# mLSTM products on quarters of the TensorE array in a two-block transformer kernel

## Chip, cores and metric

One Trainium2 chip, one of its cores. The metric is the device time of one execution in microseconds (us), the median of three; the trace is one more execution taken by the hardware profiler. TensorE (PE) does the matrix products, VectorE (DVE) and ScalarE (ACT) the element-wise work, SyncE (SP) and GpSimd (POOL) start transfers.

## The reference, cut to what matters

The program runs a first block of two layers (HGRN2 mixer, dilated attention, SwiGLU) and a second block of two hybrid layers on 512 tokens of width 1024. The change touches only the mLSTM mixer of the two hybrid layers. It has 4 heads, keys of width 64, values of width 128, and chunks of 64 tokens, so 8 chunks:

```
M_HEADS = 4; M_QK_DIM = 64; M_V_DIM = 128; M_CHUNK = 64
q, k, v = chunks(q) * (dk ** -0.5), chunks(k), chunks(v)
dC = einsum('bnhlv,bnhlk->bnhvk', v * e[..., None], k)        # update of each chunk
dn = einsum('bnhl,bnhlk->bnhk', e, k)
C_new = a[..., None, None] * C + s[..., None, None] * dC_c    # scan over the chunks
w = exp(log_d - m_t[..., None]) * einsum('bnhlk,bnhsk->bnhls', q, k)
num = einsum('bnhls,bnhsv->bnhlv', w, v) + a_inter[..., None] * einsum('bnhvk,bnhlk->bnhlv', C_prev, q)
den = sum(w, axis=-1) + a_inter * einsum('bnhk,bnhlk->bnhl', n_prev, q)
h = num / maximum(abs(den), exp(-m_t))[..., None]
```

Within a chunk the scores and weights are causal. Across chunks only the state C, n is used, so scores between tokens of different chunks are never needed.

## The kernel before

All work is written by hand, engine by engine, in plain order; semaphores tie the engines. The big weight products (`plain`, L2073) split every float32 operand into two parts of type fp32r and make three passes (`PASSES`); one step ("tick") is one 128x512 tile of PSUM tensor G over 4 k-blocks, 12 matmuls on line L2113 or L2117. Other PE work is hung into these ticks: `z_steps(T)` runs ahead of tick T and calls `window` (sliding-window attention) and `mlstm` (L2637). These small products write PSUM tensor X (four banks of 512 float32 columns) and are plain float32.

Head h of the mLSTM starts at tick 62 + 4h (`head_start`), and has stages at fixed distances from that tick (`heads_at(T, after)`), on PE:

- after 0: mask through the identity (L2662, bf16) and row maxima (L2665, fp32r) into X bank 0, 512 columns each ("exponents"); then the **scores**, L2668: four matmuls 128x128x128, keys by queries of 128 tokens, into bank 1. Two heads share the 128 rows of the key tile `tmp[:, 4 or 6, :]`. `q_alone` (DVE, L1854) multiplies the pair's queries by a column `q8` that is 1/8 on the own head's 64 rows and 0 on the other head's.
- after 1: decay rows into bank 0 (L2672). DVE multiplies weights with scores (L1873) and queries with decays (L1877).
- after 2: the **updates**, L2682: seven matmuls, 64 tokens of the chunk as contraction (array rows 0-63 for even chunks, 64-127 for odd ones), both heads' 128 key columns, 129 value columns. Even chunks go to bank 0 or 1 and odd ones to bank 2 (`m_bank`).
- after 3: DVE runs the scan over the chunks into `m_state` (L1883, L1886).
- after 4: the **output** into banks 2 and 3 (`out_view`). First the weighted values, L2651: four matmuls 128x129 over 128 tokens. Then the states, L2654: seven matmuls with all 128 rows as contraction and 64 query columns, on array columns 0-63 and 64-127 in turn.
- after 5: ACT squares the output (L1098), DVE makes the norm (L1894 to L1901); after 6 PE transposes (L2344); after 7 DVE finishes the head (L1907, "done").

Since head h+1 starts four ticks after head h, stage 4 of h and stage 0 of h+1 fall on the same tick; before the change the code puts the output first. `n.take(s)` waits for the next signal of another engine, `n.own(s)` for one's own, `n.give(ins, s)` makes `ins` signal.

Of the kernel before, what the change touches and what calls it, by code (L numbers as in the profile page):

```python
# [18 lines left out]
ALU = mybir.AluOpType  # L19
AX = mybir.AxisListType.X  # L20

P = 128
# [3 lines left out]
TB = S // P  # L26
# [19 lines left out]
def constants():  # L46

    r = np.arange(P)
    f = {}
# [12 lines left out]
    q8 = np.zeros((P, 2))  # L62
    q8[:64, 0] = q8[64:, 1] = M_DK ** -0.5
    f["q8"] = q8
# [119 lines left out]
def build(nc, a, out, where1, where2, where3, stop=None):  # L184
# [12 lines left out]
    with ctx:  # L197
# [49 lines left out]
        with ExitStack() as room:  # L247
# [46 lines left out]
                                             "output", "squares", "variance", "std", "normed", "transposed", "done")}  # L294
# [8 lines left out]
        ident, ones, halves, freq, sign, q8 = (c1(k) for k in ("ident", "ones", "half", "freq", "sign", "q8"))  # L303
# [83 lines left out]
        def keys_of(i):  # L387

            return (i - 1, i) if i else (0,)

# [838 lines left out]
        def _(dve):  # L1229
# [622 lines left out]
            def q_alone(h):  # L1852

                n.give(ts(tmp[:, 1, :], z_qm[:, h // 2, :], q8[:, h % 2:h % 2 + 1], None, ALU.mult), ms["q_alone"])  # L1854

            def k_end(h):
                pr = h // 2
                for j in range(TB):
                    ins = ts(tmp[:, 3, blk(j)], z_km[:, j, pr * P:(pr + 1) * P], mcol[:, 16 + 4 * j + h:17 + 4 * j + h], None, ALU.mult)
                n.give(ins, ms["k_end"])  # L1860

            def mlstm(T, l):
# [6 lines left out]
                for h in heads_at(T, 1):  # L1869
                    W = tmp[:, (0, 5)[h % 2], :]  # L1870
                    n.take(ms["weights_exp"])
                    n.take(ms["scores"])
                    n.give(tt(W, W, X[:, 1, :], ALU.mult), ms["weights"])  # L1873
                    qs = tmp[:, (2, 7)[h % 2], :]
                    n.take(ms["decay"])
                    n.own(ms["q_alone"])
                    n.give(tt(qs, tmp[:, 1, :], X[:, 0, :], ALU.mult), ms["q_decayed"])  # L1877
                    if h + 1 < M_HEADS:
                        n.own(ms["q_decayed"])
                        q_alone(h + 1)  # L1880
                for h in heads_at(T, 3):
                    n.take(ms["updates"])
                    link(v.tensor_copy(m_state[:, 0, :], X[:, 0, 0:P + 1]))  # L1883
                    for c in range(1, 7):
                        bank, i = m_bank(c)
                        ins = stt(m_state[:, c, :], m_state[:, c - 1, :], mcol[:, 48 + 8 * h + c:49 + 8 * h + c],  # L1886
                                  X[:, bank, (P + 1) * i:(P + 1) * (i + 1)], ALU.mult, ALU.add)
# [157 lines left out]
        def _(pe):  # L2045
# [591 lines left out]
            def mlstm(T):  # L2637
# [8 lines left out]
                for h in heads_at(T, 4):  # L2646
                    n.take(ms["states"])
                    n.take(ms["done"] if h else ws["done"])
                    W, qs = tmp[:, (0, 5)[h % 2], :], tmp[:, (2, 7)[h % 2], :]
                    for j in range(TB):  # L2650
                        mm(out_view[:, j, 0:P + 1], W[:, blk(j)], z_vm[:, j, h, :], start=j % 2 == 0, stop=False, skip_group_check=True)  # L2651
                    for c in range(1, 8):
                        r = slice(64 * (c % 2), 64 * (c % 2) + 64)
                        ins = mm(out_view[r, c // 2, 0:P + 1], qs[:, 64 * c:64 * c + 64], m_state[:, c - 1, :],  # L2654
                                 start=False, stop=c == 7, skip_group_check=True)
                    n.give(ins, ms["output"])
                for h in heads_at(T, 0):
                    pr = h // 2
                    if h == 0:
                        n.take(ms["columns_copied"])  # L2660
                        n.take(ms["k_copied"])
                    mm(X[:, 0, :], identb, mk("ml", 0, 512), start=True, stop=False)  # L2662
                    if h == 0:
                        n.take(ms["rows_selected"])
                    n.give(mm(X[:, 0, :], sel_max[:, blk(h)], rows_r[:, :], start=False, stop=True), ms["exponents"])  # L2665
                    n.take(ms["q_alone"])
                    for j in range(TB):
                        ins = mm(X[:, 1, blk(j)], tmp[:, (4, 6)[pr], blk(j)], tmp[:, 1, blk(j)], start=True, stop=True, skip_group_check=True)  # L2668
                    n.give(ins, ms["scores"])
                for h in heads_at(T, 1):  # L2670
                    n.take(ms["weights_exp"])
                    n.give(mm(X[:, 0, :], sel_decay[:, blk(h)], rows_r[:, :], start=True, stop=True), ms["decay"])  # L2672
                for h in heads_at(T, 2):
# [5 lines left out]
                    for c in range(7):  # L2679
                        r = slice(64 * (c % 2), 64 * (c % 2) + 64)  # L2680
# [141 lines left out]
```

## Time and profile before

| | us |
|---|---|
| median of three | 3033.14 |
| lowest, highest | 3032.38, 3034.7 |
| the profiled execution | 3033.12 |
| its span, first to last instruction | 3031.4 |

The granted TensorE clock is 1.000 (2.4 GHz) over the span. In a row of the timeline come the start, the time from the first start to the last end, engine, line, operation, output and inputs, rows*columns of the array used, the output's shape and type, and how many records are merged. A float32 matmul leaves two records of MATMUL and two of LDWEIGHTS, an fp32r or bf16 one leaves one of each. Records of successive matmuls overlap because their drain is counted, so what a matmul costs is the distance between starts, not its duration. The mask products of L2662 have LDWEIGHTS records but no MATMUL ones.

### The profile page before, as it was taken

What the parts mean: (1) busy time and instruction counts of PE and PEld (TensorE: products, weight loads), DVE (VectorE), ACT (ScalarE), POOL (GpSimd) and SP (SyncE); (2) the same over time, 40 slices, a digit from 0 to 9 for tenths busy, and PEclk for the clock granted to TensorE, in tenths of its full rate; (3) what the DMA queues carried; (4) which work ended last, traced back from release to release, by engine and by line L of the source; (5) the groups of instructions that cost most, each with busy time, mean ns of one, the idle gap of its engine ahead of it and who ended that gap; (6) DMA issues with size and microseconds to landing.
All of it is one profiled execution on the core that took longest, in us unless ns stands there. A gap on an engine that the chain in (4) does not pass through costs nothing.

```text
span 3031.4 us, 39648 instructions
## 1 busy us (share of the span) xinstructions
PE 2998.4 (99%) x16986; PEld 2531.0 (83%) x17002; DVE 1558.9 (51%) x2161; ACT 1135.9 (37%) x1686; POOL 30.3 (1%) x44
## 2 busy tenths in 40 slices
PE   8999999999999999999999999999999999999999
PEld 7888988888987777988889777888889877898887
DVE  7776654645255565623336765653334655663341
ACT  5654422225232333522224456342233455442231
POOL 0000000000000000000000000000000000000000
PEclk9999999999999999999999999999999999999999
DMA  8433354532322221233322222232222222222222
GB/s 299 165 114 110 115 204 154 177 133 84 96 85 70 70 80 61 70 97 98 98 93 82 84 70 70 72 107 96 97 94 86 84 84 70 79 88 98 97 98 83
DMA packets 218909, 311.59 MB, mean 103 GB/s; under 512 B 12048, under 2 KB 119024, under 8 KB 218736
## 3 DMA queue, kind: packets, MB, share of 16 engines
q1 hardware_dynamic: 207520, 267.01, 27.4%
q0 software_dynamic: 10880, 41.95, 3.9%
q8 instruction: 134, 2.20, 0.3%
q14 instruction: 39, 0.32, 0.0%
q10 hardware_dynamic: 336, 0.12, 0.0%
HBM read 306.93 MB, written 2.10 MB: 102 GB/s over the span
## 4 chain that ended last, share of the span: by engine, by line
PE 91%; DVE 7%; ACT 1%; issue 1%; ACTq 0%; DMA 0%; DVEq 0%
PE G L2113 62%; PE G L2156 9%; PE G L2117 7%; DVE yT L1625 1%; PE X L2221 1%; PE X L2504 1%; DVE w_lo L1247 1%; PE G L2135 1%; PE X L2603 1%; PE X L2518 1%; PE X L2613 1%; PE G L2375 1%; PE X L2338 1%; PE X L2515 1%; PE G L2560 1%
## 5 line engine op out<-in xcount | busy, mean ns | idle before, releaser
L2113 PE MATMUL G<-u_hi,w_hi 128*128 128x512 f32 x2128 | 847.5, 398 | 0.5 <-issue 0.5
L2113 PE MATMUL G<-u_hi,w_lo 128*128 128x512 f32 x2128 | 829.8, 390 | 0.0
L2113 PE MATMUL G<-u_lo,w_hi 128*128 128x512 f32 x2128 | 829.4, 390 | 0.0
L1247 DVE TENSOR_TENSOR w_lo<-raw,w_hi 128x2048 fp32r<-128x2048 f32 (+3 forms) x240 | 540.3, 2253 | 483.3 <-ACT w_hi L643 482.5
L643 ACT CAST w_hi<-raw 128x2048 fp32r<-128x2048 f32 (+3 forms) x242 | 454.5, 1880 | 536.1 <-DMA raw<-in_w_ff 243.7
L2113 PEld LDWEIGHTS G<-u_hi,w_hi 128*128 128x128 f32 x2128 | 399.7, 188 | 88.3 <-issue 8.3
L2113 PEld LDWEIGHTS G<-u_hi,w_lo 128*128 128x128 f32 x2128 | 399.4, 188 | 85.5
L2113 PEld LDWEIGHTS G<-u_lo,w_hi 128*128 128x128 f32 x2128 | 400.1, 188 | 79.6 <-issue 1.4
L2113 PE MATMUL G<-ff_hi,w_lo 128*128 128x512 f32 x384 | 149.4, 389 | 0.0
L2113 PE MATMUL G<-ff_hi,w_hi 128*128 128x512 f32 x384 | 149.4, 389 | 0.0
L2113 PE MATMUL G<-ff_lo,w_hi 128*128 128x512 f32 x384 | 149.4, 389 | 0.0
L2156 PE MATMUL G<-u_hi,w_hi 128*128 128x256 f32 x512 | 147.3, 288 | 1.1 <-DVE yT L1358 1.1
L2156 PE MATMUL G<-u_lo,w_hi 128*128 128x256 f32 x512 | 144.8, 283 | 0.0
L2156 PE MATMUL G<-u_hi,w_lo 128*128 128x256 f32 x512 | 144.8, 283 | 0.0
L2117 PE MATMUL G<-w_hi,u_hi 128*128 128x512 f32 (+1 forms) x352 | 136.4, 388 | 0.0
L2117 PE MATMUL G<-w_lo,u_hi 128*128 128x512 f32 (+1 forms) x352 | 134.9, 383 | 0.0
L2117 PE MATMUL G<-w_hi,u_lo 128*128 128x512 f32 (+1 forms) x352 | 134.8, 383 | 0.0
L1983 DVE TENSOR_TENSOR hid_f<-silu_g,G 128x512 f32<-128x512 f32 x44 | 30.1, 689 | 184.8 <-PE G L2113 178.5
L2032 DVE TENSOR_TENSOR sq_f<-relu_f 128x512 f32<-128x512 f32 x64 | 44.1, 692 | 146.7 <-ACT relu_f L1212 146.5
L1284 DVE SCALAR_TENSOR_TENSOR acc<-ada_raw,cond,acc 128x512 f32<-128x512 f32 x140 | 105.3, 752 | 11.2 <-DMA ada_raw<-in_ada_w 2.9
L2113 PE MATMUL G<-hid_hi,w_hi 128*128 128x512 f32 x272 | 106.1, 390 | 0.0
L1212 ACT ACTIVATE relu_f<-G 128x512 f32<-128x512 f32 x64 | 38.0, 597 | 181.1 <-PE G L2113 165.9
(459 smaller groups left out, 4505.5 us busy)
## 6 DMA issues: line engine op xcount, KB each, us to landing
raw<-in_w_ff SPq DMA_DIRECT2D x128, 512.0 KB, 4.4
raw<-in_ffn_w_in SPq DMA_DIRECT2D x88, 512.0 KB, 4.6
ada_raw<-in_ada_w POOLq DMA_DIRECT2D x40, 1024.0 KB, 6.6
raw<-in_w_in SPq DMA_DIRECT2D x56, 512.0 KB, 4.5
raw<-in_attn_w_in SPq DMA_DIRECT2D x96, 256.0 KB, 3.8
raw<-in_ffn_w_out SPq DMA_DIRECT2D x40, 512.0 KB, 4.7
raw<-in_hgrn_w_in SPq DMA_DIRECT2D x32, 512.0 KB, 4.7
raw<-in_attn_w_in SPq DMA_DIRECT2D x24, 512.0 KB, 4.3
```

Of the source, the lines that this page charges most:

```text
L643: sc.copy(w_hi[slot][:, 0:nk, 0:w], raw[slot][:, 0:nk, 0:w]).then_inc(s_hi, 1)
L1212: evicted(g, b, m, lambda: sc.activation(fold(relu_f[:, m % 2, :]), summed_tile(name, b, m), ACT.Relu))
L1247: tt(w_lo[slot][:, 0:nk, 0:w], raw[slot][:, 0:nk, 0:w], w_hi[slot][:, 0:nk, 0:w].bitcast(F32), ALU.subtract).then_inc(s_lo, 1)
L1284: ins = stt(acc, ada_raw[:, s, k, :], c, acc, ALU.mult, ALU.add)
L1625: ins = stt(hg_state[:, c + 1, :], hg_state[:, c, :], decay[:, h, c:c + 1], X[:, c % 4, blk(c // 4)], ALU.mult, ALU.add)
L2032: tt(sq_f[:, m % 2, :], relu_f[:, m % 2, :], relu_f[:, m % 2, :], ALU.mult).then_inc(s_ff, 1)
L2113: ins = mm(G[0:c1_ - c0, m, :], w[iw][:, k, c0:c1_], xs[ix][:, x0(b) + kk, :], start=first, stop=last, skip_group_check=True)
L2117: ins = mm(G[:, m, o0:o1], tokens(xs[ix][:, kk, :], tok), w[iw][:, k, c0:c1_], start=first, stop=last, skip_group_check=True)
L2135: ins = mm(G[:, m, :], w[iw][:, k, blk(m)], xs[ix][:, x0(b) + k, :], start=(k, iw, ix) == (0, 0, 0), stop=(k, iw, ix) == (3, 1, 0), skip_g ...
L2156: ins = mm(half_tile(hf, m), w[iw][:, k, m * P:m * P + P], xs[ix][:, kk, half[hf]], start=m % 2 == 0 and kk == 0 and (iw, ix) == (0, 0), s ...
L2221: ins = mm(X[:, bank, SUM_COLS * j:SUM_COLS * j + SUM_COLS], sq[:, blk(j)], ones[:, 0:SUM_COLS], start=start and j == 0, stop=True, skip_g ...
L2338: ins = mm(X[:, 3, SUM_COLS * q:SUM_COLS * q + SUM_COLS], accs[:, i % 2, blk(q)], ones[:, 0:SUM_COLS], start=True, stop=True, skip_group_c ...
```

## The change

Scores are made by chunk: eight matmuls of 64 key tokens by 64 query tokens, on the own head's 64 array rows, with even chunks on array columns 0-63 and odd ones on 64-127. The weighted values are eight matmuls with the 64 tokens of one chunk as contraction, each on one quarter of the array on its diagonal. The states take the own head's 64 rows only. Updates load only the own head's 64 key columns. `q_alone`, the decayed queries and the scan work on the 64 partitions of the own head, `k_end` on 64 columns instead of 128, and `q8` goes. On the shared tick the scores of head h+1 now come ahead of the output of head h, and the wait for the states stands ahead of the mask product.

In the output the chunks are ordered by which quarter they use: first the weighted values of the chunks whose parity is not the head's ("across"), then those of the other four ("along"), then the states of the along chunks, and then, behind a wait for the across values (semaphore `intra`), the states of the across chunks.

```
             def k_end(h):
-                pr = h // 2
                 for j in range(TB):
-                    ins = ts(tmp[:, 3, blk(j)], z_km[:, j, pr * P:(pr + 1) * P], ...)
+                    ins = ts(tmp[:, 3, 64 * j:64 * j + 64], z_km[:, j, 64 * h:64 * h + 64], ...)
...
-                for h in heads_at(T, 4):
-                    n.take(ms["states"])
-                    n.take(ms["done"] if h else ws["done"])
-                    W, qs = tmp[:, (0, 5)[h % 2], :], tmp[:, (2, 7)[h % 2], :]
-                    for j in range(TB):
-                        mm(out_view[:, j, 0:P + 1], W[:, blk(j)], z_vm[:, j, h, :], start=j % 2 == 0, stop=False, skip_group_check=True)
-                    for c in range(1, 8):
-                        r = slice(64 * (c % 2), 64 * (c % 2) + 64)
-                        ins = mm(out_view[r, c // 2, 0:P + 1], qs[:, 64 * c:64 * c + 64], m_state[:, c - 1, :], ...)
-                    n.give(ins, ms["output"])
                 for h in heads_at(T, 0):
+                    if h:
+                        n.take(ms["states"])
...
-                    for j in range(TB):
-                        ins = mm(X[:, 1, blk(j)], tmp[:, (4, 6)[pr], blk(j)], tmp[:, 1, blk(j)], start=True, stop=True, skip_group_check=True)
+                    own = m_half(h)
+                    for c in range(8):
+                        tok = slice(64 * c, 64 * c + 64)
+                        ins = mm(X[m_half(c), 1, tok], tmp[own, (4, 6)[h // 2], tok], tmp[own, 1, tok], start=True, stop=True,
+                                 skip_group_check=True, tile_position=(64 * (h % 2), 64 * (c % 2)))
                     n.give(ins, ms["scores"])
+                for h in heads_at(T, 4):
+                    if h == M_HEADS - 1:
+                        n.take(ms["states"])
+                    n.take(ms["done"] if h else ws["done"])
+                    own, W, qs = m_half(h), tmp[:, (0, 5)[h % 2], :], tmp[:, (2, 7)[h % 2], :]
+                    across, along = [c for c in range(8) if (c + h) % 2], [c for c in range(8) if (c + h) % 2 == 0]
+                    for c in across + along:
+                        r = m_half(c)
+                        ins = mm(out_view[r, c // 2, 0:P + 1], W[r, 64 * c:64 * c + 64], z_vm[r, c // 2, h, :], start=c % 4 < 2, stop=c == 0,
+                                 skip_group_check=True, tile_position=(64 * (c % 2), 64 * (c % 2)))
+                        if c == across[-1]:
+                            n.give(ins, ms["intra"])
+                    for c in along + across:
+                        if c == across[0]:
+                            n.own(ms["intra"])
+                        if c:
+                            ins = mm(out_view[m_half(c), c // 2, 0:P + 1], qs[own, 64 * c:64 * c + 64], m_state[own, c - 1, :],
+                                     start=False, stop=True, skip_group_check=True, tile_position=(64 * (h % 2), 64 * (c % 2)))
+                    n.give(ins, ms["output"])
...
-                        ins = mm(X[:, bank, (P + 1) * i:(P + 1) * (i + 1)], tmp[r, 3, blk(c // 2)], z_vm[r, c // 2, h, :],
-                                 start=True, stop=True, skip_group_check=True)
+                        ins = mm(X[m_half(h), bank, (P + 1) * i:(P + 1) * (i + 1)], tmp[r, 3, 64 * (c // 2):64 * (c // 2) + 64], z_vm[r, c // 2, h, :],
+                                 start=True, stop=True, skip_group_check=True, tile_position=(64 * (c % 2), 64 * (h % 2)))
                     n.give(ins, ms["updates"])
```

(`m_half(i)` is the slice of 64 rows that starts at 64 * (i % 2).) On PE, the tick that output of head 0 and scores of head 1 share, before:

```order
L2113 MATMUL G<-u_hi,w_lo 128x512
L2651 MATMUL X<-z_vm,tmp 128x129 x4
L2654 MATMUL X<-m_state,tmp 64x129 x7
L2662 MATMUL X<-masks 128x512
L2665 MATMUL X<-split_rows,select_maximum 128x512
L2668 MATMUL X<-tmp 128x128 x4
L2113 MATMUL G<-u_hi,w_hi 128x512
```

The same tick after (L2654 is now the mask product, L2662 the scores, L2673 the weighted values, L2681 the states):

```order
L2115 MATMUL G<-u_hi,w_lo 128x512
L2654 MATMUL X<-masks 128x512
L2657 MATMUL X<-split_rows,select_maximum 128x512
L2662 MATMUL X<-tmp 64x64 x8
L2673 MATMUL X<-z_vm,tmp 64x129 x8
L2681 MATMUL X<-m_state,tmp 64x129 x7
L2115 MATMUL G<-u_hi,w_hi 128x512
```

The exponents and scores moved ahead of the output, and four plus four full-array products became eight plus eight on quarters.

## Rows read from the trace of the kernel before

**Rows 1.** The page: busy time and share of each engine; the chain by engine
```profile
PE 2998.4 (99%) x16986; PEld 2531.0 (83%) x17002; DVE 1558.9 (51%) x2161; ACT 1135.9 (37%) x1686; POOL 30.3 (1%) x44
PE 91%; DVE 7%; ACT 1%; issue 1%; ACTq 0%; DMA 0%; DVEq 0%
```

**Rows 2.** Groups of PE by shape: records, busy us, mean ns, idle before
```profile
L2682 PE MATMUL X<-z_vm,tmp 64*128 64x129 f32 x112 | 9.2, 287 | 0.0
L2654 PE MATMUL X<-m_state,tmp 128*64 128x129 f32 x112 | 8.8, 280 | 0.0
L2651 PE MATMUL X<-z_vm,tmp 128*128 128x129 f32 x64 | 8.6, 277 | 0.8 <-DVE yT L1907 0.8
L2668 PE MATMUL X<-tmp 128*128 128x128 f32 x64 | 8.4, 275 | 0.0
```

**Rows 3.** Timeline of PE: output of head 0, scores of head 1
```profile
1845.83 0.39 PE L2113 MATMUL G<-u_hi,w_lo 128*128 128x512 f32 x1
1846.06 1.05 PE L2651 MATMUL X<-z_vm,tmp 128*128 128x129 f32 x8
1847.04 1.10 PE L2654 MATMUL X<-m_state,tmp 128*64 128x129 f32 x14
1848.11 0.58 PE L2665 MATMUL X<-split_rows,select_maximum 128*128 128x512 f32 x1
1848.53 1.05 PE L2668 MATMUL X<-tmp 128*128 128x128 f32 x8
1849.34 0.48 PE L2113 MATMUL G<-u_hi,w_hi 128*128 128x512 f32 x1
1849.66 0.39 PE L2113 MATMUL G<-u_lo,w_hi 128*128 128x512 f32 x1
```

**Rows 4.** Timeline of PE: updates of head 0 between two ticks
```profile
1839.07 0.39 PE L2113 MATMUL G<-u_hi,w_lo 128*128 128x512 f32 x1
1839.38 1.16 PE L2682 MATMUL X<-z_vm,tmp 64*128 64x129 f32 x14
1840.47 0.50 PE L2113 MATMUL G<-u_hi,w_hi 128*128 128x512 f32 x1
1840.81 0.39 PE L2113 MATMUL G<-u_lo,w_hi 128*128 128x512 f32 x1
```

**Rows 5.** Timeline of PE in stretches of 0.02 to 0.04 us
```profile
1839.38 0.49 PE L2682 MATMUL X<-z_vm,tmp 64*128 64x129 f32 x4
...
118.23 0.32 PE L2469 MATMUL X<-yT,hg_q 128*32 128x128 f32 x4
```

**Rows 6.** Timeline of PE: output of head 3, which has no scores behind it
```profile
1897.59 1.13 PE L2651 MATMUL X<-z_vm,tmp 128*128 128x129 f32 x8 [0.39 <-DVE yT L1907]
...
1900.01 0.39 PE L2113 MATMUL G<-u_lo,w_hi 128*128 128x512 f32 x1
```

**Rows 7.** Timeline of PE: narrow products in other stages
```profile
24.08 1.95 PE L2359 MATMUL G<-cond,hg_f 128*128 128x64 f32 x16
...
889.31 0.70 PE L2504 MATMUL X<-at_qk 128*32 128x128 f32 x24
...
1831.62 0.66 PE L2613 MATMUL X<-tmp,z_v 128*64 128x128 f32 x8
```

**Rows 8.** Waits of PE from 1820 to 1900 us: total, times, longest
```profile
PE X L2344 <- DVE yT L1901: 1.6, 3, 0.7
PE X L2651 <- DVE yT L1907: 0.4, 1, 0.4
```

**Rows 9.** Timeline from 1852 us: the norm of head 0 on DVE
```profile
1852.61 0.69 DVE L1877 TENSOR_TENSOR tmp<-tmp,X 128x512 f32<-128x512 f32 x1 [2.02 <-PE X L2672]
...
1853.74 0.16 DVE L1894 TENSOR_SCALAR stat<-X 128x4 f32<-128x4 f32 x1
...
1855.17 0.69 DVE L1901 TENSOR_TENSOR yT<-X,stat 128x512 f32<-128x512 f32 x1
...
1856.01 0.63 PE L2344 MATMUL X<-con,yT 128*128 128x128 f32 x4 [0.70 <-DVE yT L1901]
```

More of the change, by code:

```diff
@@ L293, in build @@
                                              "q_alone", "k_end", "scores", "decay", "weights", "q_decayed", "updates", "states",
-                                             "output", "squares", "variance", "std", "normed", "transposed", "done")}
+                                             "intra", "output", "squares", "variance", "std", "normed", "transposed", "done")}
         ws = {k: sem("window_" + k) for k in ("q_squares", "k_squares", "q_sums", "k_sums", "q_std", "k_std", "q_scaled", "q_rotated", "k_rotated", "k_ready",
@@ L302, in build @@
         c1 = lambda k: con1[:, where1[k][0]:where1[k][1]]
-        ident, ones, halves, freq, sign, q8 = (c1(k) for k in ("ident", "ones", "half", "freq", "sign", "q8"))
+        ident, ones, halves, freq, sign = (c1(k) for k in ("ident", "ones", "half", "freq", "sign"))
         mk = lambda k, lo, hi: masks[:, where3[k][0] + lo:where3[k][0] + hi].bitcast(BF16)
@@ L389, in keys_of, with m_half @@
             return (i - 1, i) if i else (0,)
+        def m_half(i):
+            return slice(64 * (i % 2), 64 * (i % 2) + 64)
         def m_bank(c):
@@ L1852, in q_alone @@
             def q_alone(h):
-                n.give(ts(tmp[:, 1, :], z_qm[:, h // 2, :], q8[:, h % 2:h % 2 + 1], None, ALU.mult), ms["q_alone"])
+                own = m_half(h)
+                n.give(ts(tmp[own, 1, :], z_qm[own, h // 2, :], M_DK ** -0.5, None, ALU.mult), ms["q_alone"])
             def k_end(h):
-                pr = h // 2
                 for j in range(TB):
-                    ins = ts(tmp[:, 3, blk(j)], z_km[:, j, pr * P:(pr + 1) * P], mcol[:, 16 + 4 * j + h:17 + 4 * j + h], None, ALU.mult)
+                    ins = ts(tmp[:, 3, 64 * j:64 * j + 64], z_km[:, j, 64 * h:64 * h + 64], mcol[:, 16 + 4 * j + h:17 + 4 * j + h], None, ALU.mult)
                 n.give(ins, ms["k_end"])
@@ L1876, in mlstm @@
                     n.own(ms["q_alone"])
[L1877 removed]
+                    n.give(tt(qs[m_half(h), :], tmp[m_half(h), 1, :], X[m_half(h), 0, :], ALU.mult), ms["q_decayed"])
                     if h + 1 < M_HEADS:
@@ L1882, in mlstm @@
                     n.take(ms["updates"])
-                    link(v.tensor_copy(m_state[:, 0, :], X[:, 0, 0:P + 1]))
+                    own = m_half(h)
+                    link(v.tensor_copy(m_state[own, 0, :], X[own, 0, 0:P + 1]))
                     for c in range(1, 7):
                         bank, i = m_bank(c)
-                        ins = stt(m_state[:, c, :], m_state[:, c - 1, :], mcol[:, 48 + 8 * h + c:49 + 8 * h + c],
-                                  X[:, bank, (P + 1) * i:(P + 1) * (i + 1)], ALU.mult, ALU.add)
+                        ins = stt(m_state[own, c, :], m_state[own, c - 1, :], mcol[own, 48 + 8 * h + c:49 + 8 * h + c],
+                                  X[own, bank, (P + 1) * i:(P + 1) * (i + 1)], ALU.mult, ALU.add)
                         if c < 6:
@@ L2645, in mlstm @@
                     transposes(X[:, 3, :], lambda j: yT[:, 4 + h, blk(j)], TB, ms["transposed"])
-                for h in heads_at(T, 4):
-                    n.take(ms["states"])
-                    n.take(ms["done"] if h else ws["done"])
-                    W, qs = tmp[:, (0, 5)[h % 2], :], tmp[:, (2, 7)[h % 2], :]
-                    for j in range(TB):
-                        mm(out_view[:, j, 0:P + 1], W[:, blk(j)], z_vm[:, j, h, :], start=j % 2 == 0, stop=False, skip_group_check=True)
-                    for c in range(1, 8):
-                        r = slice(64 * (c % 2), 64 * (c % 2) + 64)
-                        ins = mm(out_view[r, c // 2, 0:P + 1], qs[:, 64 * c:64 * c + 64], m_state[:, c - 1, :],
-                                 start=False, stop=c == 7, skip_group_check=True)
-                    n.give(ins, ms["output"])
                 for h in heads_at(T, 0):
-                    pr = h // 2
-                    if h == 0:
+                    if h:
+                        n.take(ms["states"])
+                    else:
                         n.take(ms["columns_copied"])
```

6 lines of the change are left out of this document (2 added, 4 removed).

## The prediction

> **What bounds the kernel.** I read the page's busy shares and chain first. PE is busy 99% of the span and makes 91% of the chain that ended last, DVE 51% and ACT 37% busy [rows 1]. So a change pays or costs what it does to the length of PE's own stream, plus what it does to the few waits of PE. Next come the groups by shape: the four kinds of product that the change rewrites hold 112 + 112 + 64 + 64 records in both layers together [rows 2]. Their busy times overlap and can't be added, so the cost is read from distances between starts. Output and scores of one shared tick take from 1846.06 to 1849.66, where the second big product behind them starts: 3.60 us [rows 3]. Updates take from 1839.38 to 1840.81, 1.43 us [rows 4]. Eight heads (four in each of two layers) make some 40 us, 1.3% of the time; the effect is confined to that.
>
> **The unit.** Eight float32 records of the full array (L2651) last 1.05 us from first start to last end, one alone about 0.28, so they start (1.05 - 0.28) / 7 = 0.11 us apart [rows 2, 3]. I call 0.11 us a round. Products on different parts of the array share rounds. Four records of L2682 have started 0.24 us after the first one, in two rounds; seven products on two row halves in turn, 14 records, span (1.16 - 0.27) = 0.89 us between first and last start, 8 rounds and not 14 [rows 4, 5]. L2654 does the same on two column halves, 14 records in 8 rounds (1.10 us with the last drain) [rows 3]. On four column quarters of L2469, four records start within 0.04 us [rows 5]. So before the change the scores cost 8 rounds, the weighted values 8, the states 8, the updates 8. All of these take neighbours in the program from different parts of the array; that is the point at which the new code differs.
>
> **Scores.** Eight products of 64 columns on two column halves in turn: 16 records in 8 rounds again, but of what length? The rows bound it. Above: 64 columns streamed with a full 128-column load still take (1.95 - 0.28) / 15 = 0.11 us a record in L2359 [rows 7], no gain. Below: L2504 has, at its first tile, 2 rounds of 128 columns and 4 rounds of 32 columns on four quarters; 24 records start within 0.70 - 0.24 = 0.46 us, and less 2 x 0.11 this leaves 0.06 us for each narrow round [rows 7]. The new loads are 64 wide, between the two; two such loads run side by side in L2613, whose 8 records take 4 rounds, 0.66 us [rows 7]. I take 0.06, as load and stream are both halved. Scores: 8 x 0.11 = 0.88 becomes 0.48, a gain of 0.40 us a head, 0 at the other bound.
>
> **Output.** With parities, call the quarters A (the other head's rows, weighted values of the across chunks), B (own rows, values and then states of the along chunks) and C (own rows, states of the across chunks). In program order PE meets A four times (8 records), B four times (8), B three or four times more (6 or 8), C four or three times (8 or 6): runs on one quarter, no turns. If the quarters' runs overlap, A and B start together; A's last start is 7 rounds in, its results are complete 0.27 us later, and PE sees its own signal some 0.1 us after that (PE started 0.15 us after DVE's L1901 ended at 1855.86 [rows 9]; I take a little less for its own), so C begins at about round 10.5. It ends at 18.5 rounds for even heads and 16.5 for odd ones, while B is done by 14 or 16. Mean 17.5 rounds, 1.93 us, against 16 rounds, 1.76 us: 0.17 us dearer a head, the wait for `intra` being what is late. If runs don't overlap except where one ends and the next begins, the 15 products cost 30 records less 2 seams of 2 rounds, 26 rounds, 2.86 us; if not even there, 30 rounds, 3.30 us. Then `intra` has long been signalled and costs nothing.
>
> **Updates.** Same turns between row halves, 129 columns streamed, so 8 rounds stay. The first round of the group is longer, since the second half's load isn't hidden; with a 64-column load it should shrink: 0.89 us less 6 rounds leaves 0.23 for the first step of L2682 [rows 4], and L2613, with 64-wide loads, has (0.66 - 0.27) - 2 x 0.11 = 0.17 [rows 7]. I take 0.05 us x 8 heads.
>
> **Switches between shapes.** Before the updates PE goes from 1839.07 to 1839.38, 0.31 us instead of 0.23, and behind them 1840.47 to 1840.81, 0.34 instead of 0.23 [rows 4]. On the shared tick there was one excursion to a tiled shape (L2654) between two full ones; now scores and output form one excursion. Equal in number; I add 0.06 us, as the return now goes straight to a big product. Head 0's scores, alone on their tick, gain an excursion: about 0.34 us.
>
> **Sum.** Shared ticks, six: 3.60 us less 24 rounds (2.64) leaves 0.96 for masks, maxima and switches; after, 0.96 + 0.06 + 0.48 + 1.93 = 3.43, so -0.17 each, -1.0. Scores of head 0, two: 0.88 becomes 0.48 + 0.34, -0.06 each, -0.1. Output of head 3, two: 1897.59 to 1900.01 is 2.42 [rows 6], with 1.5 rounds more +0.17 each, +0.3. Updates -0.4. Total -1.2 us on the profiled execution's 3033.12, which is the median within 0.02: 3032 us.
>
> **Waits and the other engines.** PE waits 0.70 us at L2344 for DVE's L1901 [rows 8, 9]. This chain starts with L1877, which waits for the decay product one tick after the change's place, so it moves along with PE and stays, unless the squares of the output come late: before, they stood behind ACT's exponentials of the next head, now the exponentials are earlier and the output ends later. It ended at 1847.04 + 1.10 = 1848.14 [rows 3], and would end at about 1849.4 in case 1 and 1850.3 in case 2, while DVE comes to its statistics (L1894) only at 1853.74 [rows 9]; so I take the squares to stay hidden. The 0.4 us before the output of head 3 [rows 8] hangs on DVE's L1907 and stays. DVE gets 64 columns in `k_end` and 64 partitions elsewhere; DVE isn't waited for there, so I cost this at nothing, and if that cover were gone it would be worth some 0.2 us a head.
>
> **What the Trainium skill says.** The trace shows the first half of the fourth product in flight within 0.04 us of the first one's, over the waiting second halves of three products [rows 5]. The Trainium skill (TensorE: Matmul & The Clock Gate, The mechanism) states that only weight loads are pulled ahead, while matmuls are strict FIFO in start and end; by the program's order of halves the trace doesn't agree, though it may hold product by product. By that rule the output would cost the 26 rounds of the second case below. A row of L2682 has its two row halves writing different banks (`m_bank`); no row shows two row groups writing one bank at once, as A and B now do. The Trainium skill (TensorEngine Tiling (Array Packing), Gotcha 1: PSUM Pressure) states that different row tiles cannot access the same PSUM bank simultaneously; by that the third case below holds.
>
> **Rivals.** (1) *Runs overlap*, the forecast: -1.2 us; with scores at 0.11 a round 8 x 0.4 = 3.2 more, +2.0; without the wait's 2.5 rounds -3.4. For it: PE already passes over three waiting records. (2) *The look-ahead is short*: PE passes over three records, but A's run puts seven waiting ones of the same quarter ahead of B. Then 8.5 rounds more, 8 x 8.5 x 0.11 = +7.5, total +6.3 us, slower; a look-ahead of half a run gives about +3. It decides from the point at which B's first record starts no earlier than A's last product. For it: no row shows two runs on one quarter each overlapping. (3) *A and B exclude each other*, by a bank conflict or full order: 30 rounds, 8 x 12.5 x 0.11 = +11.0, total +9.8 us. (4) *The waits move*: the squares late, or the 0.7 us waits gone: +-2 us around each case.
>
> **How the numbers follow.** Case 1 has 0.45, an intermediate look-ahead 0.10, case 2 0.25, case 3 0.17, anything beyond 0.03. A measurement of this kernel can tell 0.2% (6.1 us) from no change. Case 1 and the intermediate one lie within it, with some two fifths of case 2 (scatter of 1 us around +6.3); the rest of case 2, case 3 and a little else are slower; only a PE gain beyond everything computed here would be faster by 6. So faster 0.02, same 0.62, slower 0.36. The forecast is case 1, 3032.0 us. The range runs from -3.6 (case 1 without the wait for `intra`) to +10.4 us (case 3 with half of the scores' gain gone): 3029.5 to 3043.5.
>
> **What would show it.** Right: values and states of one head, 30 records, start within some 1.9 us, A's and B's records in pairs; scores' 16 records within 0.5 us; updates unchanged at 0.9. Case 2: 30 records over 2.8 us with single starts but for two seams; case 3: 3.2 us. Scores over 0.9 us would refute the halved round. A longer wait at L2344's successor would mean that the squares became late. Wrong altogether if the big products themselves changed their 0.23 us.

## The result

The changed kernel takes 3038.75 us (median of 20 runs, 3036.53 to 3041.68) against 3034.02 us for the kernel before in the same comparison. The ratio is 1.0017, with a 95% interval of 1.0011 to 1.0023: slower by 5.2 us, between 3.3 and 7.0 (4.7 by the two medians). One of the 20 executions of the kernel before was in a slow state (3292.4 us) and is left out of the ratio. The time is inside the stated range and within the 0.2% that the text took as no change, but clear of noise, and on the other side of zero than the forecast of -1.2 us.

The page of the changed kernel, busy times and chain by engine, to be held against [rows 1]:

```profile
PE 3002.5 (99%) x17114; PEld 2531.5 (83%) x17130; DVE 1558.2 (51%) x2161; ACT 1136.4 (37%) x1686; POOL 30.3 (1%) x44
PE 89%; DVE 7%; ACT 1%; DMA 1%; issue 1%; ACTq 0%; SPq 0%; POOLq 0%; DVEq 0%
```

PE stays the bound and has 128 more records. The shared tick of output 0 and scores 1, timeline of PE (start, length, engine, line, operation, operands, shape, records), answers to [rows 3]:

```profile
1846.77 0.39 PE L2115 MATMUL G<-u_hi,w_lo 128*128 128x512 f32 x1
1847.04 0.58 PE L2657 MATMUL X<-split_rows,select_maximum 128*128 128x512 f32 x1
1847.55 0.68 PE L2662 MATMUL X<-tmp 64*64 64x64 f32 x16
1848.07 1.54 PE L2673 MATMUL X<-z_vm,tmp 64*64 64x129 f32 x16
1849.45 1.32 PE L2681 MATMUL X<-m_state,tmp 64*64 64x129 f32 x14
...
1851.04 0.40 PE L2115 MATMUL G<-u_lo,w_hi 128*128 128x512 f32 x1
```

From the start of the last big product ahead to that of the second one behind it took 3.83 us before (1845.83 to 1849.66) and takes 4.27 now (1846.77 to 1851.04). I call this distance the stretch of the tick; it contains 0.46 us (two steps of 0.23) that are there without the small products, and the expectations below count without them, so 3.37 before and 3.81 now. The 16 score records start within 0.68 - 0.22 = 0.46 us, as forecast. Values and states, 30 records, start from 1848.07 to 1849.45 + 1.32 - 0.27 = 1850.50, 2.43 us: 23 rounds of 0.11, not 17.5.

Why, is seen in three short stretches of the same timeline (1848.48 to 1848.50, 1848.53 to 1848.56 and 1849.68 to 1849.70):

```profile
1848.29 0.38 PE L2673 MATMUL X<-z_vm,tmp 64*64 64x129 f32 x2
...
1848.29 0.55 PE L2673 MATMUL X<-z_vm,tmp 64*64 64x129 f32 x4
...
1849.45 0.55 PE L2681 MATMUL X<-m_state,tmp 64*64 64x129 f32 x4
```

Until 0.43 us after the first start only one record starts per round; just behind, two are started at once. The quarter B begins with the fifth record of A's eight, so four of 30 records find a partner at the seam from A to B. The seam from B to C is the same: B has six records of states in head 0, and C's first one starts with B's third, 0.23 us after B's first, when B has four left. So 30 records take 30 - 4 - 4 = 22 rounds. The 23rd is lost at the seams, where the second record of the new quarter comes 0.16 us behind its first instead of 0.11.

Head 3's output with its wait, and the waits of PE from 1820 to 1905 us (total, times, longest), answer to [rows 6, 8]:

```profile
1899.13 0.39 PE L2115 MATMUL G<-u_hi,w_lo 128*128 128x512 f32 x1
1900.26 1.56 PE L2673 MATMUL X<-z_vm,tmp 64*64 64x129 f32 x16 [0.74 <-DVE yT L1909]
1903.24 0.40 PE L2115 MATMUL G<-u_lo,w_hi 128*128 128x512 f32 x1
...
PE X L2346 <- DVE yT L1903: 1.8, 3, 0.7
PE X L2673 <- DVE yT L1909: 0.7, 1, 0.7
```

The wait ahead of this output grew from 0.39 to 0.74 us. Put together for the first of the two layers (the second comes to the same within 0.1 us), each term as the forecast had it and as the two timelines have it:

| term, us a layer | forecast | trace |
|---|---|---|
| three shared ticks | -0.5 | +1.33 |
| scores of head 0 | -0.06 | -0.07 |
| output of head 3, without its wait | +0.17 | +0.56 |
| four updates | -0.2 | -0.24 |
| waits of PE for DVE | 0 | +0.57 |
| sum | -0.6 | +2.15 |

Two layers make +4.3 us. The profiled spans differ by 5.8 us; of this, 1.06 lie ahead of the first mLSTM head (the maxima of head 0 start at 1832.25 before and at 1833.31 after), in stretches that the change doesn't touch, and 0.3 between the mLSTM stages of the two layers, 626 us long. What is left, 4.4, fits the sum. The 4.3 us agree with the 3.3 to 7.0 of the timed runs.

### The profile page after: what moved, and what is told of

Same layout as the page of the kernel before. It is cut to its first block, busy times and chain, and to the rows that moved or that the text cites. A ratio compares the mean times of both kernels' runs of the same rounds, so it can differ in the third digit from the quotient of the medians.

```text
span 3037.2 us, 39898 instructions
## 1 busy us (share of the span) xinstructions
PE 3002.5 (99%) x17114; PEld 2531.5 (83%) x17130; DVE 1558.2 (51%) x2161; ACT 1136.4 (37%) x1686; POOL 30.3 (1%) x44
## 4 chain that ended last, share of the span: by engine, by line
PE 89%; DVE 7%; ACT 1%; DMA 1%; issue 1%; ACTq 0%; SPq 0%; POOLq 0%; DVEq 0%
PE G L2115 61%; PE G L2158 9%; PE G L2119 7%; DVE yT L1626 1%; PE X L2223 1%; PE X L2506 1%; DVE w_lo L1248 1%; PE G L2137 1%; DMA ada_raw<-in_ada_w 1%; PE X L2605 1%; PE X L2520 1%; PE X L2615 1%; PE X L2517 1%; PE G L2562 1%; DVE acc L1285 0%
## 5 line engine op out<-in xcount | busy, mean ns | idle before, releaser
L2115 PE MATMUL G<-hid_lo,w_hi 128*128 128x512 f32 x272 | 105.8, 389 | 0.0
```

Of the source, the lines that this page charges most:

```text
L2115: ins = mm(G[0:c1_ - c0, m, :], w[iw][:, k, c0:c1_], xs[ix][:, x0(b) + kk, :], start=first, stop=last, skip_group_check=True)
```

## Experiments

### What costs the rounds: order within the output

Two theories stood against each other. A, B and C are the quarters as the prediction names them. Theory 1: PE passes over at most four records of one quarter, as if each quarter had a short queue, so a longer run of products on one quarter keeps the next quarter waiting. Theory 2: A and B cannot write one PSUM bank at the same time.

**Values in turns.**

```
-                    for c in across + along:
+                    for c in range(8):
```

> The changed kernel, with the weighted values in the order of the chunks (0 to 7), so that quarters A and B take turns; the order of the states stays. Theory 1 (short look-ahead: PE passes over at most four waiting records of one quarter): the 16 records of the values start within 8 rounds, 0.78 us from first to last start instead of 1.27; of the states, C can start only about 0.37 us after A's last start (the wait for intra), at about round 11, and ends at about round 19, so values and states start within about 2.0 us instead of 2.43 a head, and the time falls by 8 x 0.43 = 3.4 us against the changed kernel. Theory 2 (two row halves cannot write one PSUM bank at once): chunks 0 and 1 write bank 2 from both row halves, so the values take 16 rounds, 1.65 us, and the time rises by about 3 us against the changed kernel.

Timeline of PE, the same tick, and in the last row the values of head 3:

```profile
1847.30 0.39 PE L2115 MATMUL G<-u_hi,w_lo 128*128 128x512 f32 x1
...
1848.08 0.51 PE L2662 MATMUL X<-tmp 64*64 64x64 f32 x10
1848.37 0.32 PE L2673 MATMUL X<-z_vm,tmp 64*64 64x129 f32 x1
1848.42 0.28 PE L2662 MATMUL X<-tmp 64*64 64x64 f32 x4
1848.53 0.27 PE L2673 MATMUL X<-z_vm,tmp 64*64 64x129 f32 x1
1848.54 0.22 PE L2662 MATMUL X<-tmp 64*64 64x64 f32 x2
1848.60 0.93 PE L2673 MATMUL X<-z_vm,tmp 64*64 64x129 f32 x13
...
1851.06 0.40 PE L2115 MATMUL G<-u_lo,w_hi 128*128 128x512 f32 x1
...
1899.28 1.10 PE L2673 MATMUL X<-z_vm,tmp 64*64 64x129 f32 x16 [0.70 <-DVE yT L1909]
```

The values start within 1.00 us here (1848.37 to 1849.37), and within 1.10 - 0.27 = 0.83 us where nothing runs ahead of them (head 3, the last row). The stretch is 3.76 us instead of 4.27. Chunks 0 and 1 write the same bank from both row halves and share their rounds, so theory 2 falls. The rows also show the queues to be separate for each quarter: the first value starts when ten of the 16 score records have started, over six that wait, three in each of two other quarters. Median 3034.99 us; ratio to before 1.0002 (0.9992 to 1.0012). By the medians it is 1.1 us above before where the changed kernel is 4.7: a gain of 3.7 us, where theory 1 asked for 3.4.

**Values in runs of two and of three.**

```
-                    for c in across + along:
+                    for c in across[:2] + along[:2] + across[2:] + along[2:]:      # v_runs2
+                    for c in across[:3] + along[:3] + across[3:] + along[3:]:      # v_runs3
```

> The changed kernel, with the values in runs of two products (A A B B A A B B), states as they are. Theory 1: a run is four records, just what the look-ahead passes over, so B starts with A or half a round later and the values take 8 to 9 rounds, 0.8 to 0.9 us. A rival within theory 1, that PE passes over one product only (two records) of a quarter: B starts two rounds late, 10 rounds or more, 1.0 us. Theory 2: 16 rounds, 1.65 us.

> The changed kernel, with the values in runs of three products, then one each (A A A B B B A B). In the changed kernel, with runs of four (8 records), B started 4 rounds after A; with runs of two it started with A. If the queue of a quarter holds four records, the running one among them, B starts when A has four left of six, 2 rounds or 0.22 us after A, and the 16 records take about 10 rounds, 1.0 us from first to last start. If PE instead counted all waiting records of the program, not those of one quarter, the fourth product of A could not start before B's run is nearly through, and it would be 12 rounds, 1.2 us, or more.

Timeline of PE, values of head 0; first v_runs2, with the row of the stretch 1849.12 to 1849.13 between:

```profile
1849.09 1.10 PE L2673 MATMUL X<-z_vm,tmp 64*64 64x129 f32 x16
...
1849.09 0.33 PE L2673 MATMUL X<-z_vm,tmp 64*64 64x129 f32 x2
```

and v_runs3, with the row of the stretch 1847.03 to 1847.04:

```profile
1846.81 1.32 PE L2673 MATMUL X<-z_vm,tmp 64*64 64x129 f32 x16
...
1846.81 0.55 PE L2673 MATMUL X<-z_vm,tmp 64*64 64x129 f32 x4
```

With runs of two, A and B are both in flight within 0.04 us, and the 16 records start within 1.10 - 0.27 = 0.83 us. With runs of three, the third and fourth record start together, 0.22 us after the first, and all start within 1.05 us. With runs of four (the changed kernel) B starts 0.45 us after A. So B begins when A has four records left, the running one among them: 8 - 4 = 4 rounds, 6 - 4 = 2, 4 - 4 = 0. The stretches are 3.83 and 4.06 us. The delay of four rounds was known when theory 1 was set up; those of two and of none it forecast. Both kernels were executed once, so only their traces are read, not their times. Every product here makes two records, so the runs don't tell a limit of four records from one of two products, nor from one on the weight loads that go with them.

**States in turns too.** One product on B, the wait for `intra`, then C and B alternately:

```
-                    for c in along + across:
-                        if c == across[0]:
+                    al, ac = [c for c in along if c], [c for c in across if c]
+                    turns = al[:1] + [c for i in range(4) for c in ac[i:i + 1] + al[i + 1:i + 2]]
+                    for c in turns:
+                        if c == ac[0]:
                             n.own(ms["intra"])
```

> As v_turns, and the states in turns too: one product on B, then the wait for intra, then C and B alternately. Theory 1: 8 rounds for the values, C from round 10.5 or 11 because of the wait, then 8 rounds: 18.5 to 19 rounds, 1.95 to 2.0 us, equal to v_turns within 0.05 us a head; what is left above the 16 rounds of the kernel before is the wait. Theory 2: 16 rounds for the values and 8 for the states, 24 or more, no gain against the changed kernel.

The stretch is 3.76 us for even heads, as in v_turns, and 3.54 for odd ones (3.71 in v_turns). Median 3033.16 us, ratio 0.9998 (0.9988 to 1.0007). As expected for even heads; the loss of the changed kernel is gone, and what remains in an even head is mostly the wait for `intra`: in head 0, A's last record starts at 1849.56 and C's first at 1849.89, 0.33 us later, while B has only two records of states to fill the time.

### One part alone

**The new output in the kernel before.**

```
-                        mm(out_view[:, j, 0:P + 1], W[:, blk(j)], z_vm[:, j, h, :], start=j % 2 == 0, stop=False, skip_group_check=True)
+                        ins = mm(out_view[r, c // 2, 0:P + 1], W[r, 64 * c:64 * c + 64], z_vm[r, c // 2, h, :], ...)     # c in across + along
...
-                        ins = mm(out_view[r, c // 2, 0:P + 1], qs[:, 64 * c:64 * c + 64], m_state[:, c - 1, :], ...)
+                            ins = mm(out_view[m_half(c), c // 2, 0:P + 1], qs[own, 64 * c:64 * c + 64], m_state[own, c - 1, :], ...)     # along + across
```

> The kernel before with the new output alone (values and states on quarters, runs A B B C), output ahead of the next head's exponents as before, scores and updates on the full width, VectorE on 128 partitions. If the output's runs are the cause of the whole loss: each of the eight outputs takes 7 rounds more, 0.77 us, so the shared tick costs about 4.15 us instead of 3.37 and the time is 6.2 us above before, more than the whole change. If the order on the tick or VectorE's halves were the cause, it would be under 3 us.

```profile
1845.83 0.39 PE L2117 MATMUL G<-u_hi,w_lo 128*128 128x512 f32 x1
1846.14 1.59 PE L2657 MATMUL X<-z_vm,tmp 64*64 64x129 f32 x16
1847.57 1.32 PE L2665 MATMUL X<-m_state,tmp 64*64 64x129 f32 x14
...
1850.41 0.39 PE L2117 MATMUL G<-u_lo,w_hi 128*128 128x512 f32 x1
```

The stretch is 4.58 us, 0.75 above before, the 7 rounds. PE's wait ahead of head 3's output is 0.38 us, as before. Median 3039.33 us, ratio 1.0019 (1.0010 to 1.0029), 5.4 us above before by the medians, where 6.2 was expected. By the traces the output alone costs 0.75 us in each of six ticks and 0.57 in each of the two last outputs, 5.6 us, more than the 4.3 of the whole change; by the times the two can't be told apart.

**The new scores in the kernel before.**

```
-                        ins = mm(X[:, 1, blk(j)], tmp[:, (4, 6)[pr], blk(j)], tmp[:, 1, blk(j)], ...)
+                        ins = mm(X[64 * (c % 2):64 * (c % 2) + 64, 1, tok], tmp[own, (4, 6)[pr], tok], tmp[own, 1, tok], ...,
+                                 tile_position=(64 * (h % 2), 64 * (c % 2)))     # c in range(8)
```

> The kernel before with the scores by chunk alone (16 records of 64 columns on the own head's rows), all else as before. In the changed kernel these 16 records start within 0.46 us instead of 0.78 for 8, yet head 0's tick, where they are an excursion of their own, became only 0.07 us cheaper. Theory 1a (each excursion to quarters costs about 0.25 us, whatever it holds): all eight heads gain 0.07 us, 0.6 us in all, not measurable in the time, and the shared tick costs 3.30 us instead of 3.37. Rival (the switch is paid once per tick): the shared ticks gain 0.3 us each, 1.9 us in all.

The stretch is 3.74 us (1847.83 to 1851.57), 0.08 below before: the 16 records start within 0.46 us instead of 0.78 for eight, 0.32 less, so 0.24 is lost elsewhere in the stretch. What is new there beside the records is the change of shape and back, and I put it down to that. Theory 1a holds. Ratio 0.9996 (0.9987 to 1.0005), not to be told from no change, as expected.

**The order alone.** Exponents and scores of the next head ahead of the output, all products on the full array or on halves as before.

```
-                for h in heads_at(T, 4):
-                    n.take(ms["states"])
...
                 for h in heads_at(T, 0):
+                    if h:
+                        n.take(ms["states"])
...
+                for h in heads_at(T, 4):
+                    if h == M_HEADS - 1:
+                        n.take(ms["states"])
```

> Before, with exponents and scores of the next head ahead of the output on the shared tick, all products as before. The order alone: the shared tick costs 3.37 us plus or minus 0.1 (same products, one excursion, now left for a big product); exponentials on ScalarE 2 us earlier, squares later, PE's wait of 0.70 us for the norm unchanged. Time within 1 us of before. If the order were what lengthens the waits of the changed kernel, the wait ahead of head 3's output would be 0.7 us here instead of 0.39.

```profile
1846.55 0.39 PE L2113 MATMUL G<-u_hi,w_lo 128*128 128x512 f32 x1
...
1849.11 1.10 PE L2670 MATMUL X<-m_state,tmp 128*64 128x129 f32 x14
...
1850.47 0.39 PE L2113 MATMUL G<-u_lo,w_hi 128*128 128x512 f32 x1
```

The stretch is 3.92 us, 0.09 to 0.10 above before, for the same products. What differs is where the tiled shape is left, now for a big product (the second big product starts at 1850.47, 1.36 us after the first of the 14 records, whose eight rounds take 0.88) and no longer for the masks. The wait ahead of head 3's output is 0.39 us. The order costs 0.1 us a tick, 0.6 us in all, and doesn't lengthen waits. This kernel too was executed once, and only its trace is read.

### The longer waits

DVE ahead of head 3's output. Before:

```profile
1893.59 0.68 DVE L1946 TENSOR_TENSOR gate<-gate,G 128x512 f32<-128x512 f32 x1
1894.19 0.29 DVE L1883 COPY m_state<-X 128x129 f32<-128x129 f32 x1
1894.51 2.27 DVE L1886 SCALAR_TENSOR_TENSOR m_state<-m_state,mod,X 128x129 f32<-128x129 f32 x6
1896.70 0.74 DVE L1907 SCALAR_TENSOR_TENSOR yT<-X,cols_a,z_om 128x512 f32<-128x512 f32 x1
```

After:

```profile
1895.98 0.68 DVE L1948 TENSOR_TENSOR gate<-gate,G 128x512 f32<-128x512 f32 x1
1896.69 0.30 DVE L1885 COPY m_state<-X 64x129 f32<-64x129 f32 x1
1897.02 2.31 DVE L1888 SCALAR_TENSOR_TENSOR m_state<-m_state,mod,X 64x129 f32<-64x129 f32 x6
1899.36 0.75 DVE L1909 SCALAR_TENSOR_TENSOR yT<-X,cols_a,z_om 128x512 f32<-128x512 f32 x1
```

The same chain without a wait for another engine takes 3.11 us from its first to its last start before and 3.38 after. The step from the gate to the copy, now on 64 partitions, is 0.71 us instead of 0.60. From the start of the scan to L1909, back on 128 partitions, it is 2.34 instead of 2.19, and 0.11 to 0.12 of this 0.15 lie behind the last step of the scan: L1909 starts 0.03 us after the scan's end, where L1907 started 0.08 before it.

What matters isn't that the instructions have 64 partitions, but where these start. Head 3 works on partitions 64 to 127. Head 2 of the changed kernel works on 0 to 63:

```profile
1874.82 2.28 DVE L1248 TENSOR_TENSOR w_lo<-raw,w_hi 128x2048 fp32r<-128x2048 f32 x1
1877.02 0.28 DVE L1885 COPY m_state<-X 64x129 f32<-64x129 f32 x1
1877.33 2.22 DVE L1888 SCALAR_TENSOR_TENSOR m_state<-m_state,mod,X 64x129 f32<-64x129 f32 x6
1879.48 0.73 DVE L1909 SCALAR_TENSOR_TENSOR yT<-X,cols_a,z_om 128x512 f32<-128x512 f32 x1
```

Here the step into the copy is 2.20 us, as before the change (2.19 to 2.20 for heads 1 and 2), and the scan to L1909 takes 2.15, a little less than the 2.19 before. For head 1, again on 64 to 127, the same two steps are 2.31 and 2.34. Both layers show the same. So in this chain DVE starts the next instruction 0.11 to 0.12 us later where the first partition changes between 0 and 64, and not where only their number does. The waits for the norm come from the same place. For head 2, the statistics (L1896) start 0.72 us after the decayed queries of head 3, which lie on 64 to 127; before it was 0.60. Ahead of head 0's norm the reading is less simple. L1856 and L1896 both start at partition 0, yet L1896 starts 0.03 us after the other's end instead of 0.09 before it; the last instruction that read PSUM ahead of it (L1878, head 1) had started at 64. Whether that earlier one counts, no run separates.

 dve_full gives all 128 partitions, and with them the start at 0, back to every head (the column `q8` returns with them):

```
-                n.give(ts(tmp[own, 1, :], z_qm[own, h // 2, :], M_DK ** -0.5, None, ALU.mult), ms["q_alone"])
+                n.give(ts(tmp[:, 1, :], z_qm[:, h // 2, :], q8[:, h % 2:h % 2 + 1], None, ALU.mult), ms["q_alone"])
...
-                    n.give(tt(qs[m_half(h), :], tmp[m_half(h), 1, :], X[m_half(h), 0, :], ALU.mult), ms["q_decayed"])
+                    n.give(tt(qs, tmp[:, 1, :], X[:, 0, :], ALU.mult), ms["q_decayed"])
...
-                    own = m_half(h)          # the scan over the chunks
+                    own = slice(0, P)
```

> The changed kernel, but q_alone, the decayed queries and the scan of the states work on all 128 partitions as before (the other head's rows of these tiles hold values that nothing reads). Theory 3 (a VectorE instruction on 64 partitions cannot start while one on 128 still drains, and the reverse, about 0.11 us a change): PE's wait ahead of head 3's output falls from 0.74 to 0.39 us, those for the norm from 0.75 to 0.70 and from 0.30 to 0.18, so 0.57 us a layer, 1.1 us against the changed kernel, still some 3.5 us above before. Rival: the waits come from the later output, and stay at 0.74.

Waits of PE from 1820 to 1905 us:

```profile
PE X L2348 <- DVE yT L1905: 1.6, 3, 0.7
PE X L2675 <- DVE yT L1911: 0.5, 1, 0.5
```

The waits for the norm are 0.69, 0.69 and 0.17 us, as before the change, and the one ahead of head 3's output 0.45 instead of 0.74. That is 0.5 us a layer, against 0.57 expected; the shared ticks are untouched (4.28). The rival falls: the output is as late here as in the changed kernel. Theory 3 was right that DVE's steps make these waits, but put them down to the number of partitions; by head 2 it is their start. The last 0.06 us ahead of head 3 (0.45 against 0.39) weren't taken apart. Median 3037.87 us, ratio 1.0013 (1.0003 to 1.0022), 4.0 us above before where the changed kernel is 4.7; the intervals overlap, so the waits in the trace show the effect, not the time.

### Candidates for a better kernel

**One trip.** Before, in the order exponents, output as before, scores by chunk, so that the tiled products stand together.

```
+                for h in heads_at(T, 0):
...
+                    n.give(mm(X[:, 0, :], sel_max[:, blk(h)], rows_r[:, :], start=False, stop=True), ms["exponents"])
                 for h in heads_at(T, 4):
...
                 for h in heads_at(T, 0):
-                    n.give(mm(X[:, 0, :], sel_max[:, blk(h)], rows_r[:, :], start=False, stop=True), ms["exponents"])
...
-                        ins = mm(X[:, 1, blk(j)], tmp[:, (4, 6)[pr], blk(j)], tmp[:, 1, blk(j)], ...)
+                        ins = mm(X[64 * (c % 2):64 * (c % 2) + 64, 1, tok], tmp[own, (4, 6)[pr], tok], tmp[own, 1, tok], ...)
```

> A candidate for a better kernel: before, with exponents of the next head first, then the output as before (values on the full array, states on column halves in turn), then the next head's scores by chunk, right behind the states, so that they share one excursion from the full array. Theory 1a: the shared tick costs 3.37 - 0.33 = 3.04 us, head 0's scores 0.07 us less; 6 x 0.33 + 2 x 0.07 = 2.1 us below before, 3031.9 against 3034.0, ratio 0.9993. If a change between half-array and quarter-array products costs a switch of its own, 0.5 us or nothing.

```profile
1846.96 0.39 PE L2113 MATMUL G<-u_hi,w_lo 128*128 128x512 f32 x1
...
1848.63 1.09 PE L2666 MATMUL X<-m_state,tmp 128*64 128x129 f32 x14
1849.65 0.68 PE L2675 MATMUL X<-tmp 64*64 64x64 f32 x16
...
1850.60 0.40 PE L2113 MATMUL G<-u_lo,w_hi 128*128 128x512 f32 x1
```

The stretch is 3.64 us, 0.19 below before, where 0.33 was expected. A miss: halves and quarters don't share one excursion for nothing. Of the 0.14 us that are missing, 0.09 lie between them: from the last start of the states (1848.63 + 1.09 - 0.27 = 1849.45) to the first score it takes 0.20 us, where a round is 0.11. Median 3032.75 us, ratio 0.9996 (0.9987 to 1.0005), not to be told from no change.

**Cover.** From dve_full: masks and maxima, values with A and B in turns, the next head's scores, states with B and C in turns.

```
+                for h in heads_at(T, 4):
...
+                    for c in range(8):
+                        r = m_half(c)
+                        ins = mm(out_view[r, c // 2, 0:P + 1], W[r, 64 * c:64 * c + 64], z_vm[r, c // 2, h, :], ...)
...
                 for h in heads_at(T, 0):
                     n.take(ms["q_alone"])
...
                     n.give(ins, ms["scores"])
+                for h in heads_at(T, 4):
...
+                    for c in al[:1] + [c for i in range(4) for c in ac[i:i + 1] + al[i + 1:i + 2]]:
+                        if c == ac[0]:
+                            n.own(ms["intra"])
```

> A candidate that keeps the changed kernel's products on quarters but orders them by what the runs showed: masks and maxima, then the values with A and B in turns, then the next head's scores (which cover the wait for intra), then the states with B and C in turns; VectorE on all 128 partitions. One excursion and 8 rounds of 0.11, 8 of 0.058 and 8 of 0.11 us: the changed kernel's 3.81 us for the shared tick less 7 rounds is 3.04 us, 0.33 us below before; head 0's scores -0.07 and the updates -0.06 each, head 3's output about -0.1. Together 6 x 0.33 + 2 x 0.07 + 8 x 0.06 + 2 x 0.1 = 2.8 us below before, ratio 0.9991. If the short look-ahead were not what the loss comes from, the shared tick stays over 3.3 us.

```profile
1846.20 0.39 PE L2117 MATMUL G<-u_hi,w_lo 128*128 128x512 f32 x1
...
1846.99 0.77 PE L2668 MATMUL X<-z_vm,tmp 64*64 64x129 f32 x10
...
1847.82 0.56 PE L2677 MATMUL X<-tmp 64*64 64x64 f32 x10
1848.16 0.33 PE L2686 MATMUL X<-m_state,tmp 64*64 64x129 f32 x2
...
1849.53 0.40 PE L2117 MATMUL G<-u_lo,w_hi 128*128 128x512 f32 x1
```

The stretch is 3.33 us, 0.50 below before and 0.94 below the changed kernel, where only 0.33 below before was expected. Scores, values and states also overlap where they meet (states start at 1848.16 while scores are still starting), and even and odd heads cost the same (3.33 and 3.31), so the wait for `intra` is covered. Four things differ from the changed kernel at once here, and the runs don't share the gain out among them. Median 3031.24 us against 3034.47 in the same comparison; ratio 0.9990, interval 0.9981 to 0.9999. It is faster than the kernel before by 3.2 us, 0.1%, with an interval that just excludes zero; the changed kernel, measured in another comparison, is further off.

## Why the prediction was wrong

**The output** is the step that failed. It was right that only the distance between starts counts, that products on different parts of the array share rounds where they can, and that the length of the look-ahead decides. It was wrong to take case 1, unlimited overlap of the runs. The row that it rested on shows PE passing over one waiting record in each of three column quarters (L2469 in [rows 5]); it says nothing about seven in one. The measured case is the intermediate one, to which the text gave 0.10 and about +3 us: four records in each quarter's queue, 23 rounds instead of 17.5 (case 1) or 26 (case 2). For case 2 the text took each seam to save two rounds; both save four. With 23.1 - 17.5 = 5.6 rounds of 0.11 us, 0.62 us more, the forecast's -0.17 for a shared tick becomes +0.45, and the traces have +0.44. The +3 us were too low by the 1.3 rounds that the measured case has above the middle of the other two, 1.2 us, and by the waits.

**The waits** are the second failure. "DVE isn't waited for there, so I cost this at nothing" doesn't fit [rows 8]: PE waits there for L1907, and DVE's timeline has L1907 as the last of a gapless chain that holds the scan. Work on 64 partitions was taken as no slower than on 128. For the odd heads, whose partitions start at 64, that chain grew by 0.27 us, 0.23 of it at the two changes of the first partition. The wait ahead of head 3's output grew by 0.35, and with those for the norm it is 0.57 us a layer, 1.1 us of the total; the text's 0.2 us a head for this case is 0.14. A longer wait for the norm was to mean late squares. It did grow, from 0.70 to 0.75 us and from 0.18 to 0.30, but dve_full undoes this with the squares as late as ever, so that sign was read wrongly.

**Right to within 0.1 us a tick**: scores at 0.06 us a round (they start within 0.46 us), head 0's scores (-0.07, forecast -0.06), the updates (-0.06 each, forecast -0.05), the direct return to a big product (0.10, forecast 0.06), and the squares of the output, which stayed hidden. Head 3's output rose by 0.56 us where 5.6 more rounds on top of +0.17 would be 0.79. Of the 0.2 us between, 0.09 was a change of shape before: from the last start of the values to the first of the states it took 0.20 us (1897.59 + 1.13 - 0.27 = 1898.45 to 1898.65), and takes 0.11 now (1901.55 to 1901.66) that both are on quarters. The rest wasn't taken apart.

**The range** had slips of its own: case 1 without the wait is -3.4 us by the text's sum, not -3.6, and case 3 with half of the scores' gain gone is 9.8 + 1.6 = 11.4, not 10.4. The measured time is far from both ends.

**The rivals.** Case 3, the bank conflict, falls with v_turns. The Trainium skill (TensorEngine Tiling (Array Packing), Gotcha 1: PSUM Pressure) says that different row tiles cannot access the same PSUM bank simultaneously. For two row halves that write different partitions of one bank the trace shows the contrary: 16 records start within 0.83 us. The Trainium skill (TensorE: Matmul & The Clock Gate, The mechanism) has matmuls in strict order of start and end. For starts on different quarters this holds neither by record nor by product: in v_runs2 the third product of the program starts within 0.04 us of the first.

## What to carry to other kernels

Give neighbours in program order different parts of the array; here a run on one quarter blocked the next as soon as it was longer than four records (two float32 products). Smaller products gain little where the rounds stay the same (the updates 0.06 us): halve the columns that are streamed, as in the scores, not only the rows. On a chain of DVE that another engine waits for, let neighbours start at the same partition, or count 0.11 us for each change. Put work for the same shape of tiles together and let it stand between a product and the wait on its result.

## What the runs showed of the hardware

- Each quarter of the array took four records (two float32 products), the running one included, ahead of the program's order: the next quarter came 0, 2 and 4 rounds of 0.11 us late behind runs of 4, 6 and 8 records (v_runs2, v_runs3, changed kernel).
- Two row halves wrote different partitions of one PSUM bank in the same round, without a loss: 16 records within 0.83 us (v_turns, head 3).
- A trip from the full array to quarters and back cost about 0.24 us beside the products (scores_only), and the step from column halves to quarters 0.09 us more than a round (one_trip).
- Between a DVE instruction that starts at partition 0 and one that starts at 64, in either order, the step between starts was 0.11 to 0.12 us longer; between 128 partitions and 64 that both start at 0, in the scan of head 2, it was as before (changed kernel, heads 1 to 3).
